# Reordered decay grams on 32-column tiles in a gated recurrence, and an output projection whose first two blocks are begun inside the last head

## The reference, cut to what matters

```python
def step(S, xs):                      # one chunk
    qc, kc, lc, vc = xs
    b = jnp.cumsum(lc, axis=2)        # running log-forget
    diff = b[:, :, :, None, :] - b[:, :, None, :, :]
    decay = jnp.where(tri, jnp.exp(jnp.where(tri, diff, 0.0)), 0.0)
    A = jnp.einsum('bhtd,bhsd,bhtsd->bhts', qc, kc, decay)
    o = (jnp.einsum('bhts,bhsv->bhtv', A, vc)
         + jnp.einsum('bhtd,bhdv->bhtv', qc * jnp.exp(b), S))
    S = (jnp.exp(b_last)[..., None] * S
         + jnp.einsum('bhsd,bhsv->bhdv', kc * jnp.exp(b_last - b), vc))
...
o = rmsnorm(o, g_onorm).reshape(B, T, D_MODEL) * jax.nn.silu(g)
return o @ w_o, S                     # the output projection
h = h + mix
```

## Time and profile before

| what | value |
|---|---|
| profiled execution | 1781.3 us, of it the span 1779.7 us |
| median of three runs | 1781.21 us |
| PE busy (matmul) | 1709.6 us, 96% of the span |
| PE weight loads | 1619.7 us, 91% |
| DVE / ACT / POOL busy | 940.2 / 658.2 / 307.3 us |
| the chain that ended last | PE 89%, of it L1353 75% and L1380 3% |
| DMA | 171.76 MB, 97 GB/s over the span |

### The profile page before, as it was taken

One profiled execution on the slowest core, in us unless ns is written; L12 is line 12 of the kernel. 1 busy time (PEld: TensorE's weight loads), 2 busy tenths in 40 slices (PEclk: granted clock), 3 DMA queues, 4 the chain that ended last, 5 costly groups with the idle time before them and its releaser, 6 DMA issues.

```text
span 1779.7 us, 33926 instructions
## 1 busy us (share of the span) xinstructions
PE 1709.6 (96%) x12754; PEld 1619.7 (91%) x12754; DVE 940.2 (53%) x1593; ACT 658.2 (37%) x1057; POOL 307.3 (17%) x362
## 2 busy tenths in 40 slices
PE   5999999989999999999999998888899999999997
PEld 5999999969999999999999997555589999999997
DVE  5788888875455555332443434444455555554221
ACT  4544444533433333222333444333333333333111
POOL 3222222212222222000000001111012222221000
PEclk8999999989999999999999999999999999999999
DMA  4222222212222222222233352555613222222331
GB/s 173 62 81 76 72 72 74 70 51 84 87 83 82 82 82 80 82 87 86 91 116 119 97 174 73 184 186 190 197 48 87 84 82 82 82 82 82 106 92 39
DMA packets 79236, 171.76 MB, mean 97 GB/s; under 512 B 6738, under 2 KB 40802, under 8 KB 79170
## 3 DMA queue, kind: packets, MB, share of 16 engines
q1 hardware_dynamic: 73218, 149.84, 27.4%
q0 software_dynamic: 5952, 21.02, 3.4%
HBM read 158.56 MB, written 12.27 MB: 96 GB/s over the span
## 4 chain that ended last, share of the span: by engine, by line
PE 89%; DMA 3%; DVE 2%; issue 2%; ACT 1%; SPq 1%; POOL 0%; DVEq 0%; ACTq 0%; POOLq 0%
PE acc L1353 75%; PE aux L1380 3%; DMA dec_Kd<-cache_k_in 3%; PE acc L1565 2%; PE acc L1583 1%; PE aux L1597 1%; SPq L351 1%; PE aux L1513 1%; PE aux L1441 1%; PE aux L1434 1%; PE aux L1388 1%; DVE xl L713 1%; PE acc L1573 1%; PE aux L1393 1%; PE aux L1419 0%
## 5 line engine op out<-in xcount | busy, mean ns | idle before, releaser
L1353 PE MATMUL acc<-xl,w_hi 128*128 128x288 f32 x2192 | 488.0, 304 | 21.6 <-DVE w_lo L707 16.6
L1353 PE MATMUL acc<-xh,w_hi 128*128 128x288 f32 x2192 | 472.0, 297 | 0.0
L1353 PE MATMUL acc<-xh,w_lo 128*128 128x288 f32 x2192 | 471.6, 297 | 0.0
L707 DVE TENSOR_TENSOR w_lo<-w_raw,w_hi 128x1024 fp32r<-128x1024 f32 (+1 forms) x217 | 283.6, 1307 | 337.6 <-ACT w_hi L382 334.2
L1353 PEld LDWEIGHTS acc<-xl,w_hi 128*128 128x128 f32 x2192 | 355.2, 190 | 35.1 <-DVE w_lo L707 17.3
L1353 PEld LDWEIGHTS acc<-xh,w_lo 128*128 128x128 f32 x2192 | 355.8, 190 | 0.0
L1353 PEld LDWEIGHTS acc<-xh,w_hi 128*128 128x128 f32 x2192 | 355.7, 190 | 0.0
L382 ACT ACTIVATE w_hi<-w_raw 128x1024 fp32r<-128x1024 f32 (+1 forms) x217 | 224.2, 1033 | 240.3 <-PE acc L1353 206.0
L1353 PE MATMUL acc<-ffn_glo,w_hi 128*128 128x288 f32 x704 | 151.0, 295 | 0.0
L1353 PE MATMUL acc<-ffn_gh,w_lo 128*128 128x288 f32 x704 | 149.8, 293 | 0.0
L1353 PE MATMUL acc<-ffn_gh,w_hi 128*128 128x288 f32 x704 | 148.9, 293 | 0.0
(11 more groups left out here) (250 smaller groups left out, 2449.6 us busy)
## 6 DMA issues: line engine op xcount, KB each, us to landing
w_raw<-w_fi_in SPq DMA_DIRECT2D x88, 512.0 KB, 3.6
w_raw<-w_mix_in SPq DMA_DIRECT2D x32, 512.0 KB, 3.6
w_raw<-w_fo_in SPq DMA_DIRECT2D x32, 512.0 KB, 3.5
dec_Kd<-cache_k_in SPq DMA_DIRECT2D x32, 512.0 KB, 6.9
dec_Vd<-cache_v_in SPq DMA_DIRECT2D x32, 512.0 KB, 5.9
w_raw<-w_kv_in SPq DMA_DIRECT2D x17, 512.0 KB, 3.7
w_raw<-w_o_in SPq DMA_DIRECT2D x16, 512.0 KB, 3.6
w_raw<-w_qg_in SPq DMA_DIRECT2D x16, 512.0 KB, 3.6
```

The source lines that it names most:

```text
L707: nc.vector.tensor_tensor(w_lo[:, pos.slot % SPL, 0:width], w_raw[:, pos.slot, 0:width], w_hi[:, pos.slot % SPL, 0:width].bitcast(F32), AL ...
L1353: mm = nc.tensor.matmul(acc[:, tp, hf, 0:HALF], W[:, sp_, 128 * j:128 * j + 128], X[:, kt, HALF * hf:HALF * hf + HALF], start=(first and j ...
```

## The change

The eight grams change their order and their shape. The levels now go from small to large (1, 2, 4, ..., 64). k and qd (q times the forget values) are grown in place: at each level DVE multiplies half of each by a block's decay and forms the next decay by a product of two neighbours (`grow`), so the cumulated sum, the exponentials and `diff` and `zed` are gone. Grams 0 to 5 only need 32 x 32 blocks on the diagonal. PE computes them as matmuls of 32 output rows by 32 columns, four of them in the four 32-column tiles of the array (`tile_position`), the samples as a fifth chunk; grams 6 and 7 use two column tiles. `take` copies less, and `diagonal_blocks` moves the gathered 32 x 32 blocks into A. The places in `quarters` change, ACT has one exponential, `forget`, in place of nine.

At step 8 PE now runs six of the eight input tiles of the output projection's first two blocks between the last head's pieces, at step 9 the seventh; `ffn` only runs the eighth for them. The `hi` and `lo` of the second block are moved up to the head of step 8.

```diff
+            def grow(hd, rp, j):
+                m = 1 << j
+                kv, qv = level(k_[:, rp], m), level(qd[:, rp], m)
...
+                dve.wait_ge(z_ok, 8 * hd + j + 1)
...
+                nc.vector.tensor_tensor(kv[:, :, 0, :], kv[:, :, 0, :], dm_[:, :, 1:2].to_broadcast([P, n, m]), ALU.mult)
+                nc.vector.tensor_tensor(qv[:, :, 1, :], qv[:, :, 1, :], dm_[:, :, 0:1].to_broadcast([P, n, m]), ALU.mult)\
+                    .then_inc(z_ok, 1)
...
+                nc.vector.tensor_tensor(decay(rp, 2 * m).rearrange("p (n one) -> p n one", one=1)[:, 0:n],
+                                        dm_[:, :, 0:1], dm_[:, :, 1:2], ALU.mult).then_inc(dk_ok, 1)
...
             def gram(hd, rp, g):
+                pe.wait_ge(z_ok, 8 * hd + max(g, 1))
...
+                wait(pe, gram_used, 8 * hd + (0 if g == 1 else g))
+                lhs, rhs = k_[:, rp], q_[:, rp] if g == 0 else qd[:, rp]
+                if g < 6:
+                    at = 160 if g == 1 else 0
+                    for c in range(NCH + (g < 4)):
+                        for x in range(4):
+                            r, s = slice(32 * x, 32 * x + 32), CH * c + 32 * (x if c < NCH else x % 2)
+                            mm = nc.tensor.matmul(aux[r, 1, at + 32 * c:at + 32 * c + 32], lhs[:, s:s + 32], rhs[:, s:s + 32],
+                                                  start=True, stop=True, tile_position=(0, 32 * x))
...
-                for c in range(NCH):
-                    mm = nc.tensor.matmul(aux[:, g % 2, CH * c:CH * c + CH], lhs[:, CH * c:CH * c + CH],
-                                          rhs[:, CH * c:CH * c + CH], start=True, stop=True)
...
                 def state(c):
                     pe.wait_ge(vb_ok, td + 1)
+                    pe.wait_ge(og_ok, 2 * td + 2)
...
                 quarters = (
-                    {1: [(tail, outs), (tail, lambda: state(0))], 5: [(tail, onorm)]},
-                    {0: [(tail, lambda: state(1))], 3: [(rec, gram_0)], 6: [(rec, lambda: gram(hd, rp, 1))]},
...
+                    {2: [(rec, grams_01), (tail, outs)], 3: [(rec, lambda: gram(hd, rp, 2))], 5: [(rec, lambda: gram(hd, rp, 3))],
+                     6: [(tail, onorm)]},
+                    {0: [(rec, lambda: gram(hd, rp, 4))], 3: [(rec, lambda: gram(hd, rp, 5))], 4: [(tail, lambda: state(0))],
+                     6: [(rec, lambda: gram(hd, rp, 6))]},
+                    {0: [(tail, lambda: state(1))], 1: [(rec, lambda: gram(hd, rp, 7))], 4: [(rec, turn_v)], 6: [(rec, turn_k)]},
+                    {1: [(rec, ds)]})
...
+                    elif isinstance(t, int) and t == HEADS and k < 2:
+                        gemm(Pos(B_WO0 + k), T_WO0 + k, k, range(HEADS - 2), oh, ol, last=False, wait_x=(ol_ok, 0), part=True,
+                             mid={j: (lambda steps=steps: run(steps)) for j, steps in mid.items()})
...
+                    elif isinstance(t, int) and t == HEADS + 1 and k < 2:
+                        gemm(Pos(B_WO0 + k), T_WO0 + k, k, range(HEADS - 2, HEADS - 1), oh, ol, first=False, last=False,
+                             wait_x=(ol_ok, 0), j0=HEADS - 2, part=True)
...
                 for m in range(DT):
-                    gemm(Pos(b_in - 8 + m), t_in - 8 + m, (t_in + m) % 2, range(DT), rh, rl,
-                         wait_x=wait_first if m == 0 else None)
+                    done = HEADS - 1 if layer == 0 and m < 2 else 0
+                    gemm(Pos(b_in - 8 + m), t_in - 8 + m, (t_in + m) % 2, range(done, DT), rh, rl,
+                         wait_x=wait_first if m == 0 else None, first=(done == 0), j0=done)
...
                 for m in range(DT):
-                    if m or layer == 0:
+                    if m:
                         lo(Pos(b_in - 8 + m + 1))
                     add_h(m, b_in - 8 + m, (t_in - 8 + m) % 2, h_base + m + 1)
```

More of the change, by code:

```diff
@@ L1358, in gemm @@
                         mid[j]()
[L1359 removed]
+                if not part:
+                    mm.then_inc(block_done, 1)
             def norm(n, n_ssq):
```

305 lines of the change are left out of this document (141 added, 164 removed).

## The result

The changed kernel takes **1765.01 us** (median of 4 runs, 1763.12 to 1767.18) beside 1780.24 us for the kernel before on the same chip (4 runs, 1779.26 to 1783.7). The ratio is 0.991, 95% interval 0.9896 to 0.9925: 15 us faster, where 36.9 were forecast. The profiled execution took 1763.12 us (span 1761.5), so 18.2 us of span are to be placed against the profiled execution before. Forecast 1744, range 1732 to 1776: the direction and the range hold, the size does not.

The account below looks back on a forecast made before the run. PE bounds the heads, a chain through all engines the stretch behind them. Savings of 26.4 (heads 2 to 7), 5.0 (head 1) and 7.7 (end), less 2.2 ahead, take 36.9 us off 1781.3: 1744 us, range 1732 to 1776.

Parts of the forecast that it names:

- The grams, 4.0 us a head: In every head, small matmuls run four tiles side by side, so the grams take 4.0 us, 5.3 less than before.
- New waits of 0.9 in a head: In each head, grams wait for DVE's copies and products; mostly hidden, 0.9 us of new waits (0 to 3).
- A head of 38.9 us at clock 1.00.: Heads 2 to 7 take 38.9 us each at clock 1.00, 4.4 us less a head, 26.4 in all.
- Head 1, 5.0: Head 1 goes from 38.46 to 33.4 us, with about 2.0 of waits in it: 5.0 less.
- Ahead of the heads, 2.2 lost: Before head 1, the fourth block's `w_lo` stands behind q's log-sigmoid and ends at 48.7, costing 2.2 us.
- The end, 7.7 gained: From the last head to the third projection block: 43.3 us instead of 50.98, 7.7 gained (3 to 10).
- The head start lies in PE's gaps: Behind the last head, the 84 projection matmuls moved up (11.1 us) fit where PE waits.
- Rival 1: In the grams, small matmuls cannot be fed fast enough, 0.02 to 0.03 us each: 1767 us (1760 to 1778); chance 0.16.
- Rival 2: In the heads, DVE sets the grams' pace; five of seven grams wait, 2.5 us more a head: 1761 us; chance 0.14.
- Rival 3: In grams 0 to 7, tiles do not overlap, 7.2 us more a head with waits: slower, 1826 us; chance 0.11.
- Rival 4: No change: feeding limits and DVE's pace eat the heads' gain, bare `hi` and `lo` the end's; chance 0.05.

Follow-up runs that it names:

- run 1: Changed kernel with TensorE's loop over steps 2 to 7 written out as straight code: 1764.17 us, ratio 0.9889 to the kernel before.
- run 9: Changed kernel with `outs` cut in three on TensorE, each piece behind another tile, the 16 sample matmuls in two rows of 8: 1756.81 us, ratio 0.9873.
- run 12: run 11 with `outs` cut in three as well, as in run 9: 1742.54 us, ratio 0.9791 to the kernel before.
- run 6: Changed kernel with DVE's second state add, `new_state(1)`, ahead of gram 7's copy: 1763.07 us, ratio 0.9912 to the kernel before.
- run 7: Changed kernel with unread matmuls of 192 columns put into PE's waits behind the last head: 1759.06 us, ratio 0.9873 to the kernel before.
- run 5: Changed kernel with `hi` and `lo` written one block earlier in the output projection, from the third block on: 1760.88 us, ratio 0.9885.
- run 10: Changed kernel with the last head's sample state steps moved later on DVE and TensorE: 1762.99 us, ratio 0.9914 to the kernel before.
- run 3: Changed kernel with the reordered mixer alone, without the head start of the first two projection blocks: 1774.87 us, ratio 0.9949.
- run 4: Kernel before with only the head start of the first two projection blocks added, the mixer's order unchanged: 1784.46 us, ratio 1.0017.
- run 2: Changed kernel with `outs` moved two tiles earlier in one piece, ahead of grams 0 and 1: 1768.0 us, ratio 0.9914.
- run 8: Changed kernel with `outs` cut in two, the sequence's part one tile earlier, the samples' part still behind grams 0 and 1: 1764.99 us, ratio 0.9917.
- run 11: Changed kernel with the edits of run 1, run 5, run 6, run 7 (fewer unread matmuls) and run 10 together: 1750.36 us, ratio 0.9838.
- run 14: Changed kernel with 4 instead of 20 program matmuls in each of grams 0 and 1 from head 2 on, work left out: 1759.29 us, ratio 0.9888.
- run 13: Changed kernel without the 16 sample matmuls of 8 columns in `outs`, work left out: 1744.72 us, ratio 0.9805.

## Why the prediction came out right in direction and wrong in size

**Step by step.**

- *The grams, 4.0 us a head.* The mechanism is right, tiles side by side in rounds of four; the size is off by 1.1: 1.2 for grams 0 and 1 together, 0.69 for 2 and 3 each, 0.58 for 4 and 5 each, 0.57 and 0.77 for 6 and 7 give 5.1. Both terms were too cheap. A round takes 0.041 us (0.41 for ten) instead of 0.031, which is 0.6 over the 64 rounds, and going in and out takes 0.69 - 0.41 = 0.28 instead of 0.21, which is 0.5 over seven.
- *New waits of 0.9 in a head.* Too many: PE's busy time is the whole of an undisturbed head. That the two errors nearly cancel is luck: the 38.97 us of such a head stand beside the forecast 38.9, and six of them would save 26.2 (forecast 26.4).
- *"A head of 38.9 us at clock 1.00."* **This is the step that failed in the heads**: I took the clock of before, 1.00 in all heads, for the clock after, and put the loop's jump at nothing. Against 6 x 38.97 = 233.8 the six heads took 244.2, 10.4 more, a little over half of the 18.7 us that are missing. In the three heads with half clock 1.9, 2.0 and 1.8 us remain beside the jumps: 5.6. The two jumps back cost 1.64 + 1.31 = 3.0; the other three heads are 0.5, 0.8 and 0.5 us over, of which 0.4 in the first is PE's wait for issue behind grams 0 and 1. Run 1 took the stops away and run 9 the stretches, run 12 both, and the two of its heads that were read are 38.97 each, with no wait and no half clock from 86 to 320 us.
- *Head 1, 5.0.* It came to 4.9, by two errors again: the grams cost 1.1 more, and the waits came to 1.2 us instead of 2.0.
- *Ahead of the heads, 2.2 lost.* Wrong, 0.1: the mask copy (0.26 us instead of 0.69) starts 1.2 us earlier (35.66 instead of 36.87), the log-sigmoid of q that I had left at 46.67 begins at 43.98, and DVE writes the fourth block's `w_lo` from 44.65 to 45.87, not to 48.7.
- *The end, 7.7 gained.* **This step failed too**: 0.5 lost, and 2.5 more in the third block. `outs` began 31.0 us behind the last head instead of 26.6 (4.4 late), DVE's output took 10.7 us from there instead of 8.65 (2.0), and the rest 9.8 instead of 8.05 (1.8). The chain as drawn missed the wait of the first transpose for DVE's `new_state(1)`, 2.1 us (run 6: with it gone `outs` starts 2.5 us earlier); it had no change of clock in it, although show 0.87 there already and the new order has 0.85 (run 7: 3.2 us of the way and 2.5 of the block). Its price for `hi` and `lo` is right (4.34 us), bare as said. The edits of runs 5, 6, 7 and 10 together bring the way to the third block to 43.57 us in run 12, where the forecast had 43.3 for the change without them.
- *The head start lies in PE's gaps.* True only in the new order: it gains 10.7 us there (run 3) and loses 1.8 in the old one (run 4).

**The sum.** 15.8 + 4.9 - 0.1 - 0.5 - 2.5 = 17.6 of the 18.2 us between the two profiled executions; 0.6 lies in the rest of the program.

**The rivals.** Rival 1's time (1767) is nearest to what came, but not its mechanism: a gram holds the next block matmul up by under 0.6 us, not 1. Rival 2: no waits for DVE in a full head but 0.5 for `A`. Rival 3: out, 0.69 us a gram and not 2. Rival 4: no; the end's gain was gone, but `hi` and `lo` cost what the forecast had for them. What the trace of before could have told: `outs` keeps PE for 1.8 us on matmuls of 8 columns, and the change takes the wide state matmul away from behind it and sets the grams ahead of it. That this is why the clock now falls is not shown.

## What to carry to other kernels

When a change makes PE's work shorter by making it smaller, price the clock too: look at which short matmuls come to stand together, and spread them between wide ones (here 6.6 us for an order alone). A loop body that PE went back to without a stop may bring one when it grows: look at the instruction queue's packets inside the loop and at PE's first wait after a jump. And a head start belongs with the order that leaves gaps for it; measure the two parts of such a change apart as well as together.

## What the runs showed of the hardware

Each line is read from one profiled execution of each kernel named, unless it says otherwise.

- The granted clock falls to its lower level in stretches in which PE is busy all the time. With 16 matmuls of 128 rows and 8 columns in a row (1.8 us) a stretch follows within 2 us of their end in 3 to 6 of 7 steps (the changed kernel and runs 1 to 3, 5 to 8, 10 and 11), and in one with a fifth of grams 0 and 1 (run 14); without those 16 (run 13), or with them in two rows of 8 with a block tile between (runs 9 and 12), in none. All executions of runs 8 and 9 bear that out: a mean granted clock of 0.979 to 0.980 with the 16 in one row, 0.985 to 0.987 with two rows (run 10, one row and on the chip of run 9, has 0.978 to 0.984). A few stretches begin behind a stop of PE instead (runs 2 and 7, at the jump back). The kernel before has the 16 in one row and no stretch in its heads, and that is open.
- Where PE waits, unread matmuls of 192 columns raised the granted clock from 0.85 to 0.96 and gained 6.6 us by the ratios (run 7).
- 40 matmuls of 32 columns in four column tiles start within 0.41 us, 10 ns each, and still cost 0.69 us among block matmuls.
- With a loop body of 1016 matmuls (trace count) PE stood still for 1.1 to 1.8 us at each jump back (the changed kernel and the runs that keep the loop), with one of 646 it did not. The instruction queue moved 28 packets instead of 6 from 90 to 330 us, which fits a body that is fetched again in every round. Written out (run 1, 24 packets), no stop was left in that stretch.
- The releaser that the profile names for such a stop (an add to a semaphore on DVE) is not what PE waits for: run 1 has the same add and no stop.
